# A transformer chain on one core: another order for the first transfers, ten weight slots and early modulation weights in the last layer

## The reference, cut to what matters

```python
# layer -1 ("first_block"): modulation, gated linear recurrence beside dilated attention, w_out
mod = silu(c) @ w_ada + b_ada                 # 3 x 1024: shift, scale, gate
h = rms_norm(x, norm_pre) * (1 + scale) + shift
proj = h @ w_in                               # 1024 x 3072
...
# layers 0 and 1 ("second_block"): six modulation rows each, attention, then 16 experts
m = (silu(c) @ w_ada[i] + b_ada[i])           # 6 x 1024, each row 4 MB of weights
x = x + m[2] * attention(modulate(rmsnorm(x), m[0], m[1]))
h = modulate(rmsnorm(x), m[3], m[4])
aff = softmax(h @ w_router); gates, idx = top_k(aff, cap)   # 64 rows of x per expert
y = (silu(xs @ w_gate) * (xs @ w_up)) @ w_down              # per expert, 3 x 4 MB of weights
x = x + m[5] * scatter_add(gates * y)
```

## Time and profile before

| | |
|---|---|
| times of three runs | 2565.9, 2568.18, 2570.9 us (median 2568.18) |
| profiled execution | 2568.8 us, of it a span of 2567.5 us |
| PE busy / DVE / ACT / POOL | 2245.6 (87%) / 1293.6 (50%) / 981.6 (38%) / 457.2 us (18%) |
| SP's DMA queue q1 | 518.95 MB, 51.6% of 16 engines |
| granted PE clock, mean | 0.952 |

### The profile page before, as it was taken

The page is one execution under the profiler, slowest core; times in us unless marked ns, Lnnn a source line. Parts: engine busy times, 40 slices in busy tenths (PEclk is TensorE's granted clock), DMA queues, the critical chain, the costliest instruction groups (busy, mean ns, idle before and its releaser), DMA issues.

```text
span 2567.5 us, 26437 instructions
## 1 busy us (share of the span) xinstructions
PE 2245.6 (87%) x10169; PEld 1259.7 (49%) x10169; DVE 1293.6 (50%) x2319; ACT 981.6 (38%) x1604; POOL 457.2 (18%) x463
## 2 busy tenths in 40 slices
PE   4998988899989995999999998679999787777787
PEld 2443534445657443667666675446665332222222
DVE  2137533625875227998889886366662411111111
ACT  2015333212554224888888884345552100000000
POOL 0000000000111111354456531033221000000000
PEclk8999999999999997999999999889999889999999
DMA  7111511011000328899999997400014599999998
GB/s 273 66 66 66 197 66 70 33 49 66 1 1 1 133 112 325 333 366 376 373 368 375 365 374 285 165 1 1 1 67 165 236 355 405 405 406 406 406 413 338
DMA packets 92427, 546.30 MB, mean 213 GB/s; under 512 B 7791, under 2 KB 10623, under 8 KB 67598
## 3 DMA queue, kind: packets, MB, share of 16 engines
q1 hardware_dynamic: 81886, 518.95, 51.6%
q0 software_dynamic: 6144, 20.98, 3.7%
q10 hardware_dynamic: 4272, 4.69, 0.5%
HBM read 523.62 MB, written 20.97 MB: 212 GB/s over the span
## 4 chain that ended last, share of the span: by engine, by line
PE 23%; DMA 16%; DVE 11%; ACT 6%; issue 4%; POOL 1%; SPq 0%; ACTq 0%; POOLq 0%; DVEq 0%
DMA AR<-in_w_exp_gate_dram 13%; DVE RW L2001 7%; PE PS L2035 5%; PE PS L2250 5%; PE PS L660 3%; ACT AR L2089 3%; ACT RW L1993 2%; PE PS L958 2%; PE PS L871 2%; PE PS L671 2%; PE PS L2440 1%; DMA AR<-in_w_exp_down_dram 1%; DVE AR L2208 1%; PE PS L2566 1%; DMA AR<-in_w_in_odd_dram 1%
## 5 line engine op out<-in xcount | busy, mean ns | idle before, releaser
L2250 PE MATMUL PS<-AR 128*64 128x512 f32 x1536 | 376.5, 638 | 92.2 <-DMA AR<-in_w_exp_gate_dram 46.2
L2001 DVE TENSOR_TENSOR RW<-AR,RW 128x2048 fp32r<-128x2048 f32 x192 | 432.3, 2283 | 46.5 <-ACT RW L1993 46.5
L1993 ACT CAST RW<-AR 128x2048 fp32r<-128x2048 f32 x192 | 364.1, 1913 | 123.0 <-PE PS L2035 108.5
L2035 PE MATMUL PS<-RW,RX 128*96 128x512 f32 x1536 | 364.1, 396 | 4.5 <-DVE RX L2141 4.0
L2035 PEld LDWEIGHTS PS<-RW,RX 128*96 128x96 f32 x1536 | 248.5, 163 | 111.1 <-issue 5.2
L2250 PEld LDWEIGHTS PS<-AR 128*64 128x64 f32 x1536 | 115.6, 145 | 328.3 <-issue 259.8
L660 PE MATMUL PS<-AR 128*128 128x256 f32 (+5 forms) x640 | 242.9, 496 | 4.5 <-POOL AR L645 2.3
L1655 PE MATMUL PS<-AR 128*128 128x512 f32 (+1 forms) x480 | 192.7, 558 | 5.5 <-DMA AR<-in_w_in_even_dram 5.5
L2035 PE MATMUL PS<-RW,RA 128*96 128x512 f32 x768 | 185.6, 398 | 11.5 <-DVE RA L2198 11.5
L760 DVE TENSOR_REDUCE AR<-PS 128x1 f32<-128x768 f32 (+1 forms) x160 | 135.9, 849 | 115.0 <-PE PS L660 114.6
L2327 POOL DMA_INDIRECT x_rows<-AR x16 | 119.3, 7457 | 331.8 <-DVE AR L2208 268.1
(11 more groups left out here) (335 smaller groups left out, 2595.4 us busy)
## 6 DMA issues: line engine op xcount, KB each, us to landing
AR<-in_w_exp_gate_dram SPq DMA_DIRECT2D x64, 2048.0 KB, 13.6
AR<-in_w_exp_up_dram SPq DMA_DIRECT2D x64, 2048.0 KB, 21.5
AR<-in_w_exp_down_dram SPq DMA_DIRECT2D x64, 2048.0 KB, 21.7
AR<-in_w_ada_dram SPq DMA_DIRECT2D x30, 2048.0 KB, 11.2
AR<-in_w_in_dram SPq DMA_DIRECT2D x6, 2048.0 KB, 9.0
AR<-in_w_in_even_dram SPq DMA_DIRECT2D x4, 2048.0 KB, 8.0
AR<-in_w_out_dram SPq DMA_DIRECT2D x2, 2048.0 KB, 7.7
AR<-in_w_out_even_dram SPq DMA_DIRECT2D x2, 2048.0 KB, 7.7
```

Of the source, the lines that this page charges most:

```text
L1993: s.copy(pair(i)[0], raw_half(key, hf)).then_inc(*S.up("hi", l, i))
L2001: v.tensor_tensor(lo, raw_half(key, hf), hi.bitcast(F32), ALU.subtract).then_inc(*V.up("split", key, hf))
L2035: m = pe.matmul(bank(ob)[0:Mc, :], st_, mv[:, k, 512 * q_:512 * q_ + 512], start=(k0 + k == 0 and n_ == 0), stop=(k0 + k == 7 and n_ == 2))
L2250: m = pe.matmul(bank(b)[64 * q_:64 * q_ + 64, :], op, w[:, c, 512 * q_:512 * q_ + 512], start=(h == 0 and c == 0), stop=(h == 1 and c == 3 ...
```

## The change

Start. ACT issues only the four tiles of x, each on a semaphore of its own (`dx0` to `dx3`); all else goes to SP. SP issues the identity and the rows `c`, `c_2`, `c_ctx_2` first (semaphore `dc`), then the first modulation load, the former `sp_loads`, two more modulation loads, the other rows with `inv` and `positions` (`d0`, `dpos`), the fourth modulation load, two loads of `w_in`, and only then the mask, recurrence weights, norms and context (`d1`). The row turn is split in two (`pe_colc`, `pe_cols`). SP no longer waits for `d0`. ACT's wait for `d1` before the norm is gone; the waits stand now at `dve_lam_a` and `act_lam`. PE transposes chunks 0 to 3 of x between the two halves of modulation row 1 and the rest behind it; DVE does the norm between modulation rows 0 and 1.

Last layer. There are three new slots (9 on x, 10 and 11 on the norm buffers), and the experts go round ten slots. Half 0 of modulation row 3 is loaded behind the projections, half 1 and half 0 of row 4 behind unit 47 of the attention, half 1 of row 4 behind unit 63, and row 5 behind the first gate and up weights, where slots 6 and 2 come free. The attention's probability buffers move to RB0 and RB1, so POOL clears RB0 again behind the attention. The layer's gate row goes to GB[2]; the experts' small buffers move to RB0, RB1, mask and QPX.

```diff
-        two, four, six = [0, 1], [0, 1, 2, 6], [0, 1, 3, 4, 5, 2]
+        two, four, ten = [0, 1], [0, 1, 2, 6], [4, 5, 0, 1, 3, 11, 9, 6, 2, 10]
...
+                if (nm, l, e, h) == ("gate", 1, 1, 0):
+                    ada_loads(1, [5], [6, 2])
...
+        ada_loads(1, [3], [6, 2], (0,))
         for i in range(2):
             colchunk(("outo", i), T["w_out_odd_2"][0], i * 512, i * 512 + 512, two)
-        ada_loads(1, [3], [2, 3])
-        ada_loads(1, [4], [4, 7])
-        ada_loads(1, [5], [5, 2])
+        ada_loads(1, [3], [6, 2], (1,))
+        ada_loads(1, [4], [3, 7])
         expert_loads(1)
...
+            pe_colc()
+            pe_ada_mm(-1, 0, 0, 0)
+            pe_bcols()
+            pe_ada_mm(-1, 0, 1, 1)
+            pe_ada_end(-1, 0, 6, 7)
+            pe_ada_mm(-1, 1, 0, 2)
             pe_cols()
-            pe_bcols()
-            pe_ada(-1, 0, 7)
-            pe_ada(-1, 1, 6)
-            pe_hT("n1")
+            pe_hT("n1", chunks=(0, 4))
+            pe_ada_mm(-1, 1, 1, 3)
+            pe_ada_end(-1, 1, 0, 1)
+            pe_hT("n1", chunks=(4, 8))
...
             dve_ada(-1, 0)
-            dve_ada(-1, 1)
             dve_norm("n1")
+            dve_ada_row(-1, 1, 0)
+            dve_cols()
+            dve_ada_row(-1, 1, 1)
+            dve_ada_end(-1, 1)
             dve_hT("n1")
...
             act_silu()
-            S.wait_ge("d1", "x")
             act_norm("n1")
...
+            G.wait_ge("read", "pv", "o", 63)
+            g.memset(RB0, 0.0).then_inc(*G.up("rb0", 1))
             pool_outproj("outo", tmps)
...
+                if i == 0:
+                    sp_loads_c()
                 if i == 1:
                     sp_loads()
-                    Q.wait_ge("d0", "x")
+                if i == 3:
+                    sp_loads_rows()
+                if i == 6:
+                    sp_loads_late()
...
-                if key == ("gate", 1, 1, 0):
+                if key == ("gate", 1, 1, 1):
                     sp_moe(1)
...
-                if key[0:3] in (("ada", 1, 3), ("ada", 1, 4), ("ada", 1, 5)):
+                if key == ("ada", 1, 3, 0):
+                    xn_wait(Q, "no")
+                if key == ("ada", 1, 3, 1):
+                    Q.wait_ge("full", "pv", "o", 47)
+                    Q.wait_ge("upk", 3, 5)
+                    Q.wait_ge("upU", 3, 9)
+                if key == ("ada", 1, 4, 1):
                     Q.wait_ge("full", "pv", "o", 63)
+                if slot == 11 and not no:
+                    Q.wait_ge("full", "route", 1, 0)
+                if slot == 9 and not no:
+                    Q.wait_ge("xw", 1)
+                if slot == 10 and not no:
+                    idx_wait(Q, 1)
```

More of the change, by code:

```diff
@@ L246, in program @@
         LOADS, LOAD_AT, rr = [], {}, {}
-        users = [[] for _ in range(9)]
+        users = [[] for _ in range(12)]
         def add(key, src, shape, slot):
@@ L259, in colchunk, with ada_loads @@
             cyc(key, w[:, n0:n1].rearrange("(c p) n -> p c n", p=128), (w.shape[0] // 128, n1 - n0), slots)
-        two, four, six = [0, 1], [0, 1, 2, 6], [0, 1, 3, 4, 5, 2]
-        def ada_loads(l, js, slots):
+        two, four, ten = [0, 1], [0, 1, 2, 6], [4, 5, 0, 1, 3, 11, 9, 6, 2, 10]
+        def ada_loads(l, js, slots, hs=(0, 1)):
             w = T["w_ada"][0] if l < 0 else T["w_ada_2"][l]
             for j in js:
-                for h in range(2):
+                for h in hs:
                     colchunk(("ada", l, j, h), w, j * 1024 + h * 512, j * 1024 + h * 512 + 512, slots)
@@ L272, in expert_load @@
                     ada_loads(0, [5], [4, 5])
+                if (nm, l, e, h) == ("gate", 1, 1, 0):
+                    ada_loads(1, [5], [6, 2])
                 src = T[f"w_exp_{nm}_2"][l, e, h * 512:h * 512 + 512, :].rearrange("(p c) n -> p (c n)", c=4)
-                cyc((nm, l, e, h), src, (4, 1024), six if l else four)
+                cyc((nm, l, e, h), src, (4, 1024), ten if l else four)
         def expert_loads(l):
@@ L559, in hT_wait, with pe_hT @@
                 e.wait_ge("read", "hT", tag, c - 1, 0)
-        def pe_hT(tag, behind=None):
-            n = 0
+        def pe_hT(tag, behind=None, chunks=(0, 8)):
+            n = chunks[0] * len(HTP[tag])
             xn_wait(P, tag)
-            for c in range(8):
+            for c in range(*chunks):
                 for pi, (j0, nj, m_) in enumerate(HTP[tag]):
@@ L1059, in pe_cols, with dve_cols @@
             K.fill(7, "col")
-            pe.transpose(bank(7)[:, 0:NROWS], rows, ident[0:NROWS, 0:NROWS]).then_inc(*K.full("col"))
+            pe.transpose(bank(7)[:, 0:NROWS - 24], rows, ident[0:NROWS - 24, 0:NROWS - 24]).then_inc(*K.full("col"))
+        def dve_cols():
+            V.wait_ge("full", "col")
+            v.tensor_copy(COL[:, 24:NROWS], bank(7)[:, 0:NROWS - 24]).then_inc(*V.read("col"))
         def pe_bcols():
@@ L1077, in act_silu @@
         def act_silu():
-            S.wait_ge("read", "col")
+            S.wait_ge("read", "colc")
             s.activation(sa8, col("c", 0, 8), ACT.Exp, scale=-1.0).then_inc(*S.up("silu_e", "c"))
@@ L1082, in dve_silu @@
         def dve_silu():
-            V.wait_ge("full", "col")
-            v.tensor_copy(COL, bank(7)[:, 0:NROWS]).then_inc(*V.read("col"))
+            V.wait_ge("full", "colc")
+            v.tensor_copy(COL[:, 0:24], bank(7)[:, 0:24]).then_inc(*V.read("colc"))
             V.wait_ge("slz", 0)
@@ L2210, in dve_experts @@
                                                ALU.mult).then_inc(*V.read("down", l, e, hf))
-        xF1 = [AR[:, H0 + 3584 + 512 * i:H0 + 4096 + 512 * i].rearrange("p (k c) -> p k c", c=64) for i in range(2)]
-        aF1 = [AR[:, H0 + 4608 + 512 * i:H0 + 5120 + 512 * i].rearrange("p (k c) -> p k c", c=128) for i in range(2)]
-        ac1 = [AR[:, XN0 + 4096 + 512 * i:XN0 + 4608 + 512 * i] for i in range(2)]
+        xF1 = [RB0[:, 512 * i:512 * i + 512].rearrange("p (k c) -> p k c", c=64) for i in range(2)]
+        aF1 = [RB1[:, 512 * i:512 * i + 512].rearrange("p (k c) -> p k c", c=128) for i in range(2)]
+        ac1 = [mask, QPX]
         def pe_experts1():
```

67 lines of the change are left out of this document (42 added, 25 removed).

## The result

The change makes the kernel faster: 2540.77 us (median of four, 2538.42 to 2541.27) against 2569.27 us (four runs), ratio 0.9889 with a 95% interval of 0.9872 to 0.9906. The forecast was 2536 us, the range 2525 to 2551. The profiled execution took 2541.27 us with a span of 2539.8, 27.7 less than the 2567.5 before.

The account below looks back on a forecast made before the run. Transfers were taken to bound the start and the last layer, whose expert weights are a stream of bytes. 2568.8 - 22 (last layer) - 10 (start) = 2536.8 profiled, 2536 us as median; range 2525 to 2551.

Parts of the forecast that it names:

- The last layer: Expert weight stream of the last layer: begins sooner, two loads fewer, no pause; 22 us won, ends 15 and 27.
- the three new waits: Last layer's load queue: gate 1.1 waits for the router, down 0.0 for out's landing, up 1.1 for the top-k indices.
- the pause: Last layer, 2060 to 2073: DMA slows with all six slots full before any expert has run; losing it gives 8.5 us.
- The first sum: Last layer, by landings: the 96th expert load at 2527.2 against 2551.95, a gain of 24.7 us.
- the second sum: Last layer, by bytes: 10.3 us for two loads less, 8.5 for the pause, 1.9 for the earlier beginning: 20.7 us.
- a late first expert: Last layer: first gather lands later under load, PE starts up to 2 us later, small new pause; 1.5 us off.
- the signs: Last layer, after the projection's first matmul: no slice below 300 GB/s, out +90, first expert +107 to +111, last landing +568.
- The start: Kernel start: the product with w_in begins at 47.0 instead of 56.64; 10 us won, ends 6 and 13.
- (1): Last layer's gain given back: out or slots 9 to 11 late, DMA pauses 15 to 20 us; 2558 us, chance 0.09.
- (2): Last layer: ten slots also make the queue faster, 419 GB/s, 14 us more; 2522 us, chance 0.04.
- (3): Last layer's experts: PE at the low clock becomes the bound, 39.6 us per expert; 2664 us, chance 0.04.
- (4): Nothing moves: both gains are taken up by an unseen wait; 2568 us, chance 0.04.

Follow-up runs that it names:

- g16_first: Full change, but the last layer's gathers of its first four experts bring 16 rows in place of 64: 2537.6 us, ratio 0.9878.
- norm_early: Full change, with the norm of x and transposes of its chunks 0 to 3 ahead of the second modulation load's matmuls: 2543.6 us, ratio 0.9912.
- warm: norm_early with 40 transposes of the identity into a free bank ahead of the fourth modulation load's matmuls: 2543.3 us, ratio 0.9902.
- s16_all: Full change, but the 16 scatters of the last layer add 16 rows instead of 64: 2526.7 us, ratio 0.9843.
- pair: Full change, but in the last layer one gather brings two experts' rows, into partitions 0 to 63 and 64 to 127: 2522.3 us, ratio 0.9826.
- six_slots: Full change, but the last layer's experts go round six slots again: 2554.8 us, ratio 0.9938.

## Why the prediction was right, and where not

Right were the direction, the range, both places where the gain comes from and their independence. But the total of 32 us against 28.5 hides two misses in opposite directions, and that they partly cancel is luck.

**The last layer: 22 forecast, 13.6 found, below the lower end of 15.** Right were the count of loads (seven done ahead of 2014.25, two fewer behind it), the order and the landing of out, the three new waits, and that the DMA queue, once full at 2005, never runs empty. What failed is what I set against the pause. The pause itself was sized well, as "7.1 us and a bit on either side, say 8.5". By these windows of the kernel before, with the two of the earlier trace rows between them, 2056 to 2080 falls 8.9 us short of 419 GB/s:

```profile
2056.00:2060.00 4.00, 3.22 (x4) 0.50 (x2) 0.69 (x1) 0.00 (x0) 0.99 (x2) 0.50 1.05 380
...
2073.00:2080.00 7.00, 7.00 (x38) 3.01 (x36) 1.98 (x3) 0.60 (x1) 0.00 (x0) 1.00 0.91 339
```

But I took the new stream to run at its full rate in the same place. It falls 4.9 us short there, to the first four gathers: with a quarter of their rows 5.4 us come back (g16_first; 1.9 of it are bytes no longer moved, and the same windows fall only 1.5 us short). So closing the pause is worth 8.9 - 4.9 = 4.0 us and not 8.5. Nor did the first gather of the kernel before land "with DMA half empty": the share was 0.97 or more until 2066. The first sum has the same gap, 407 GB/s for the 11 transfers and three gathers behind 2014.25. With it the second sum gives 20.7 - 4.5 = 16.2, measured is 13.6; of the other 2.6 us about 1 is the rate of 406 for 407 GB/s, the rest is not located. The landing at 2551.95 is that of the 95th load and not of the 96th (PE takes up the 96th at 2556.9), so a load costs 5.33 and not 5.26 us; this shifts both ends of the difference and hardly its size. The 1.5 us that I took off for a late first expert were not needed: PE started 107.8 us behind the output projection, as 107.7 before. Of the signs, out's landing (+89.7) and the first expert matmul came as said; not so the DMA rate (slices of 2 us at 260, 272 and 293 GB/s between 2050 and 2060), the loads that PE takes up without a wait (23, not 30) and the last landing (+584.7, not +568).

**The start: 10 forecast, 13.2 found, just past the upper end of 13.** The fourth load was put at 34 us and landed by 34.5. The step that was mis-sized comes behind it: matmuls 3.0, then 3.5 to the columns, then 5.2 for the chunks, 11.8 us to w_in from 35.2. Measured were 8.8 from 34.59. I had taken the durations from a stretch in which the granted clock was 0.59 (39.87 to 56.64 us before), and the new order leaves PE fewer and shorter waits: 0.94 from 34.59 to 43.40. norm_early and warm show what the clock alone can make of this block, 4.3 us between 0.53 and 1.00. That the clock was up here is partly chance: with the same start, w_in begins up to 1.3 us later in s16_all.

**The rivals.** (1), the gain given back, happened in part and not by late slots. (2), a faster queue through depth, did not happen: from 2144 to 2500 us it is 406 GB/s with ten slots and 407 in the kernel before, with six. The rate did have room, 420, but it was in the gathers' shape, which I had waved off as "explains the lower rate" without asking why 8.39 MB take 5.9% of the engines. The ceiling of 435 GB/s that the Trainium skill gives (DMA: Bandwidth & Descriptors, Specifications) was not the thing in the way; the best long stretch, pair's, reads 421 (short windows at a share of 1.05 read 437 and 442, so single windows are good to a few per cent). (3), the low clock in the experts, did not happen: 0.93 before and after. (4) did not.

## What to carry to other kernels

Before you price a pause of the transfers, ask what else must be moved around that time: the stream that closes the pause pays for it. A window in which DMA is busy and moves little is not idle. Where a stream of weights sets the time, small transfers into 64 partitions can cost three times their bytes, and into 128 partitions about their bytes: batch two. Durations of PE from a stretch with waits are those of the lower clock; price a new order with both levels.

## What the runs showed of the hardware that was not expected

- A gather of 64 rows of 4 KB into 64 partitions costs a saturated weight stream some 1.7 us, a scatter of as many rows 1.4 us (estimates from three quarters of each), where the bytes are worth 0.6; with 128 partitions the gathers' excess goes (20.0 us in 16). The weight packets beside a gather into 64 partitions take longer, while the DMA share stays at 1.01 in each case: a share of 1.0 does not say that the engines move all they could.
- Four gathers take 4.0 us from issue to landing with the queues empty (six_slots) and 13.1 us beside the weight stream (full change).
- Ten loads queued instead of six stretch each from 25.8 to 28.5 us between issue and landing to 47.2 to 51.4 (medians of gate, up and down loads) and change neither the rate nor the latency of gathers (11.9 and 12.1 us).
- After a wait of 4.8 us the next 9.3 us of PE work took twice as long in all three groups as after filler work (clock 0.53 against 1.00, one trace each), though the groups are parted by waits of about 1 us in both.
